# A two-block transformer kernel on one Trainium2 core: transfers, splits and sums of the opening in another order, and three small reorderings behind it

## What is computed

```python
def first_block(...):
    for layer in range(DEPTH):
        h = rmsnorm(x, attn_norm[layer])
        proj = h @ w_in[layer]
        y_a = diff_attention(a_q, a_k, a_v, cos, sin, ...) @ w_a[layer]
        y_b = hgrn2_bidirectional(b_q, b_ff, b_fb, b_i, b_g, ...) @ w_b[layer]
        merged = jax.nn.sigmoid(gate_a) * y_a + jax.nn.sigmoid(gate_b) * y_b
        x = x + merged @ w_o[layer]
        h = rmsnorm(x, ffn_norm[layer])
        x = x + (jax.nn.silu(h @ w_gate[layer]) * (h @ w_up[layer])) @ w_down[layer]
    return rmsnorm(x, final_norm)

def second_block(...):
    for l in range(DEPTH):
        x = layer_norm(ALPHA * x + 0.5 * swiglu(x, ...), ...)
        x = layer_norm(ALPHA * x + hybrid_mixer(x, ...), ...)
        x = layer_norm(ALPHA * x + 0.5 * swiglu(x, ...), ...)
```

## Time and profile before

| | us |
|---|---|
| median of 3 runs (lowest, highest) | 3565.53 (3564.04, 3565.78) |
| the profiled execution's own time | 3565.41 |
| its span in the profile | 3563.6 |
| PE busy in the span | 3506.7 |
| DVE busy | 1938.5 |
| ACT busy | 1382.6 |
| POOL busy | 463.4 |

### The profile page before, as it was taken

One profiled execution on the slowest core, in us unless ns is written; L12 is line 12 of the kernel. 1 busy time (PEld: TensorE's weight loads), 2 busy tenths in 40 slices (PEclk: granted clock), 3 DMA queues, 4 the chain that ended last, 5 costly groups with the idle time before them and its releaser, 6 DMA issues.

```text
span 3563.6 us, 44557 instructions
## 1 busy us (share of the span) xinstructions
PE 3506.7 (98%) x16012; PEld 2813.2 (79%) x16012; DVE 1938.5 (54%) x2485; ACT 1382.6 (39%) x1950; POOL 463.4 (13%) x320
## 2 busy tenths in 40 slices
PE   7999999999999999999999999999999999999998
PEld 5777888888777788888888876788878887678886
DVE  6888544434988654433443487633263328873334
ACT  4555433323455443323332355432242324653323
POOL 2333010001333110001200211200020003020002
PEclk9999999999999999999999999999999999999999
DMA  3111222223111222223222211222222222122222
GB/s 110 66 65 60 106 95 94 100 94 118 66 66 66 89 95 99 95 94 112 95 94 97 92 66 58 90 94 95 99 84 100 94 95 88 48 72 98 96 94 101
DMA packets 87378, 315.42 MB, mean 89 GB/s; under 512 B 9952, under 2 KB 10592, under 8 KB 86880
## 3 DMA queue, kind: packets, MB, share of 16 engines
q1 hardware_dynamic: 84384, 305.48, 25.2%
q10 hardware_dynamic: 2880, 8.39, 0.7%
HBM read 309.64 MB, written 4.19 MB: 88 GB/s over the span
## 4 chain that ended last, share of the span: by engine, by line
PE 87%; DVE 8%; DVEq 2%; ACT 2%; issue 1%; DMA 0%; POOLq 0%; SPq 0%; ACTq 0%; POOL 0%
PE ps L1760 22%; PE ps L1762 21%; PE ps L1761 21%; PE sc L1760 5%; PE sc L1762 5%; PE sc L1761 5%; DVE w_lo L1073 2%; PE ps L1928 1%; DVE h_lo L1520 1%; PE sc L2000 1%; DVEq L1378 1%; ACT w_hi L524 1%; DVEq L1544 1%; DVE DE L1307 1%; PE ps L1853 1%
## 5 line engine op out<-in xcount | busy, mean ns | idle before, releaser
L1073 DVE TENSOR_TENSOR w_lo<-raw,w_hi 128x1024 fp32r<-128x1024 f32 x574 | 738.7, 1287 | 1116.7 <-ACT w_hi L524 1116.4
L524 ACT ACTIVATE w_hi<-raw 128x1024 fp32r<-128x1024 f32 x574 | 607.9, 1059 | 1453.9 <-PE ps L1762 782.2
L1760 PE MATMUL ps<-h_hi,w_hi 128*128 128x512 f32 x2576 | 1049.1, 407 | 25.3 <-DVE h_lo L1083 23.2
L1762 PE MATMUL ps<-h_hi,w_lo 128*128 128x512 f32 x2576 | 1005.6, 390 | 0.0
L1761 PE MATMUL ps<-h_lo,w_hi 128*128 128x512 f32 x2576 | 1005.3, 390 | 0.0
L1760 PEld LDWEIGHTS ps<-h_hi,w_hi 128*128 128x128 f32 x2576 | 484.8, 188 | 154.8 <-issue 63.0
L1762 PEld LDWEIGHTS ps<-h_hi,w_lo 128*128 128x128 f32 x2576 | 484.0, 188 | 102.9
L1761 PEld LDWEIGHTS ps<-h_lo,w_hi 128*128 128x128 f32 x2576 | 485.4, 188 | 97.7 <-issue 9.1
L1760 PE MATMUL ps<-hid_hi,w_hi 128*128 (+1 forms) x792 | 309.7, 391 | 0.0
L1762 PE MATMUL ps<-hid_hi,w_lo 128*128 (+1 forms) x792 | 308.2, 389 | 0.0
L1761 PE MATMUL ps<-hid_lo,w_hi 128*128 (+1 forms) x792 | 308.2, 389 | 0.0
(11 more groups left out here) (314 smaller groups left out, 4337.5 us busy)
## 6 DMA issues: line engine op xcount, KB each, us to landing
raw<-wts SPq DMA_DIRECT2D x574, 512.0 KB, 3.2
x<-xT SPq DMA_DIRECT2D x1, 2048.0 KB, 10.6
x<-xT ACTq DMA_DIRECT2D x1, 2048.0 KB, 8.3
parked<-x ACTq DMA_DIRECT2D x8, 256.0 KB, 2.0
x<-parked ACTq DMA_DIRECT2D x1, 2048.0 KB, 8.1
outT<-x SPq DMA_DIRECT2D x8, 256.0 KB, 2.1
mask_in<-m ACTq DMA_DIRECT2D x1, 448.0 KB, 12.5
moves<-c ACTq DMA_DIRECT2D x1, 320.0 KB, 3.4
```

The source lines that it names most:

```text
L524: act(w_hi[:, s].rearrange("p a b -> p (a b)"), raw[:, s, :], ACT.Copy).then_inc(s_whi, 1)
L1073: tt(w_lo[:, s].rearrange("p a b -> p (a b)"), raw[:, s, :], w_hi[:, s].rearrange("p a b -> p (a b)").bitcast(F32), ALU.subtract).then_inc ...
L1760: mm(out, w_hi[:, s, b, :], hi, start=start, stop=False, skip_group_check=True)
L1762: return mm(out, w_lo[:, s, b, :], hi, start=False, stop=stop, skip_group_check=True)
```

## The change

Four parts. (a) Opening: the transfers are split up and in another order, chunk 0 in two halves, x in eight tiles on two queues, constants behind them; ACT and DVE split x and weights first and take squares, lower bounds and angles afterwards; the sum of squares is taken by PE behind chunk 2 and not behind chunk 1; four matmuls on a tile of zeros run first on PE, each 128x512 in float32. (b) The front of the first block's layers, on ACT and DVE, in another order. (c) The mixer's first scores on PE ahead of the transposes of v and three fill steps. (d) The mixer's end: the last splits, one centring and a few small steps at other pairs. Scratch tiles move: `mask_in` and four new `angle` tiles lie in space of the scan's tiles.

```diff
@@ sync
+            h0 = CHUNK // 2 * P
+            eng.dma_start(raw[:, 0, 0:h0], a_wts[0][:, 0:h0]).then_inc(s_half, 16)
             eng.dma_start(par1[:], a_par1).then_inc(s_first, 16)
-            eng.dma_start(x[:], a_x).then_inc(s_x, 16)
-            with eng.Fori(0, DEPTH * (CH1 + CH2) // 2 + 1) as pair:
+            eng.dma_start(raw[:, 0, h0:], a_wts[0][:, h0:]).then_inc(s_raw[0], 16)
+            eng.dma_start(x[:, 3, :], a_x[:, 3, :]).then_inc(s_x[3], 16)
+            eng.dma_start(raw[:, 1, :], a_wts[1]).then_inc(s_raw[1], 16)
+            for k in range(4, KT):
+                eng.dma_start(x[:, k, :], a_x[:, k, :]).then_inc(s_x[k], 16)
+            eng.dma_start(epsc[:], a_c1[:, 384:389]).then_inc(s_eps, 16)
+            eng.dma_start(ones[:], a_c1[:, 128:256]).then_inc(s_ones, 16)
+            eng.dma_start(sq[0][:].bitcast(I32), a_pos.partition_broadcast(P)).then_inc(s_pos, 16)
...
+            for s in range(2):
+                eng.wait_ge(s_wlo, 2 + s + 1)
+                eng.dma_start(raw[:, s, :], a_wts[2 + s]).then_inc(s_raw[s], 16)
+            eng.dma_start(scanm[:], a_c1[:, 389:901]).then_inc(s_const, 16)
...
+            with eng.Fori(2, DEPTH * (CH1 + CH2) // 2 + 1) as pair:
@@ scalar
-            eng.dma_start(ident[:], a_c1[:, 0:128]).then_inc(s_const, 16)
...
+            for k in range(3):
+                eng.dma_start(x[:, k, :], a_x[:, k, :]).then_inc(s_x[k], 16)
...
+                    eng.wait_ge(s_pre, 1)
+                    act(small[:, 16:32], small[:, 0:16], ACT.Exp).then_inc(s_sin, 1)
+                    split_hi(1, 1)
+                    eng.wait_ge(s_eps, 16)
+                    rstd_of(0, ps[7], D_MODEL, 0)
+                    split_hi(2, 0)
...
-                split_hi(p_proj + 2, 0)
-                split_hi(p_proj + 2, 1)
+                if L == 0:
+                    eng.wait_ge(s_pre, 2)
+                    act(sin1[:], angle[2][:], ACT.Sin)
+                    act(cos1[:], angle[3][:], ACT.Sin).then_inc(s_sin, 1)
+                    eng.preload_act_table_set("natural_log_exp_and_others")
                 front_exp(0)
...
                 split_hi(p_proj + 4, 0)
-                split_hi(p_proj + 4, 1)
                 decays(0, 0)
                 decays(0, 1)
+                split_hi(p_proj + 4, 1)
@@ scalar, mixer
                     if p == PAIRS - 1:
+                        for n in chunks_done_before(PAIRS):
+                            split_chunk(in0 + n + 2)
+                            take(n)
                         for i in range(2):
                             eng.wait_ge(q_ccx, L * 2 + i + 1)
@@ gpsimd
+            eng.memset(sT[:], 0.0).then_inc(s_warm, 1)
@@ vector
+                    eng.wait_ge(s_halfh, 1)
+                    tt(w_lo[:, 0, 0:half_k]..., raw[:, 0, 0:half_k * P], ...).then_inc(s_halfl, 1)
+                    eng.wait_ge(s_first, 16)
+                    for k in range(3):
+                        h_lo_of(0, k, k, ...)
+                    eng.wait_ge(s_whi, 1)
+                    tt(w_lo[:, 0, half_k:]..., raw[:, 0, half_k * P:], ...).then_inc(s_wlo, 1)
+                    for k in range(3, KT):
+                        h_lo_of(0, k, k, ...)
+                    split_lo(0, 1)
+                    bounds()
+                    turns()
+                    bounds_out()
...
+                split_lo(p_proj + 1, 0)
+                if L == 0:
+                    angles()
+                    split_lo(1, 1)
+                first(0, 0)
...
+                front_sums(0)
+                split_lo(p_proj + 2, 1)
+                first(1, 1)
...
+                front_decay(0)
                 first(2, 0)
                 split_lo(p_proj + 3, 0)
...
                 begin(0)
+                first(3, 1)
+                split_lo(p_proj + 4, 1)
@@ vector, mixer
                 for p in range(PAIRS + 1):
+                    if p == PAIRS - 1:
+                        for n in chunks_done_before(p):
+                            split_chunk(in0 + n + 2)
                     if p < PAIRS:
                         masked_max(p)
...
-                    if p < PAIRS:
-                        inverses(p)
-                    if p == 15:
-                        short_tap(1, 1)
-                        short_tap(1, 2)
-                        short_output(0)
+                    if p == PAIRS - 1:
                         eng.wait_ge(q_ccm, L + 1)
                         for i in range(2):
                             stt(cc[:, i, :], ps[6][:], -1.0 / 256, cc[:, i, :], ALU.mult, ALU.add).then_inc(q_ccx, 1)
-                    for n in chunks_done_before(p):
-                        split_chunk(in0 + n + 2)
+                    if p < PAIRS:
+                        inverses(p)
+                    if p == PAIRS - 2:
+                        short_tap(1, 1)
+                        short_tap(1, 2)
+                    if p == PAIRS - 1:
+                        short_output(0)
+                    else:
+                        for n in chunks_done_before(p):
+                            split_chunk(in0 + n + 2)
@@ tensor
-            eng.wait_ge(s_const, 96)
+            eng.wait_ge(s_warm, 1)
+            for _ in range(4):
+                mm(ps[7][:], sT[:, 0:P], sT[:], start=True, stop=True)
...
                 for s in range(2):
                     eng.wait_ge(s_wlo, (p_proj + 1) * 2 + s + 3)
                     chunk(ps[2 + s][:], s).then_inc(s_used, 1)
+                    if s == 0:
+                        if L == 0:
+                            proj_sums()
+                        eng.wait_ge(s_lam, L + 1)
+                        mm(ps[6][:, 0:2], ones[:], small[:, 34:36], ...).then_inc(s_lamp, 1)
@@ tensor, mixer
                 fill(2)
+                scores2(0)
                 eng.wait_ge(s_bank, bank0 + IN_TILES.index(T2_V) + 3)
                 transpose4(ps[7][:], row(M, T2_V)).then_inc(q_vTp, 1)
                 fill(FILLS2[0][0] - 2)
```

More of the change, by code:

```diff
@@ L220, in build @@
         stg = [tmp(f"stg{i}", 20 + i) for i in range(4)]
-        mask_in = tmp("mask_in", 24, 2)
+        mask_in = tmp("mask_in", 8, 2)
+        angle = [tmp(f"angle{i}", 10 + i) for i in range(4)]
         squared = [tmp(f"squared{i}", 20 + i) for i in range(KT)]
@@ L594, in gate_up, with first_high @@
                 eng.preload_act_table_set("natural_log_exp_and_others")
[L596 to L605, removed]
+            def first_high(k):
+                eng.wait_ge(s_x[k], 16)
+                act(h_hi[:, k, :], x[:, k, :], ACT.Copy, scale=par(par1, 0, C_AN + k)).then_inc(s_hhi, 1)
             eng.preload_act_table_set("natural_log_exp_and_others")
-            eng.wait_ge(s_x, 16)
             for L in range(DEPTH):
@@ L612, in _ @@
                 if L == 0:
-                    for k in range(KT):
[L614 to L620, removed]
+                    half_k = CHUNK // 2
+                    eng.wait_ge(s_half, 16)
+                    act(w_hi[:, 0, 0:half_k].rearrange("p a b -> p (a b)"), raw[:, 0, 0:half_k * P],
+                        ACT.Copy).then_inc(s_halfh, 1)
+                    eng.wait_ge(s_first, 16)
+                    for k in range(3):
+                        first_high(k)
+                    eng.wait_ge(s_raw[0], 16)
+                    eng.wait_ge(s_used, 1)
+                    act(w_hi[:, 0, half_k:].rearrange("p a b -> p (a b)"), raw[:, 0, half_k * P:],
+                        ACT.Copy).then_inc(s_whi, 1)
+                    for k in range(3, 6):
+                        first_high(k)
+                    split_hi(0, 1)
+                    for k in range(6, KT):
+                        first_high(k)
+                    for k in range(KT):
+                        square(s_x[k], 16, k, k)
+                        if k == 5:
+                            split_hi(1, 0)
+                    eng.wait_ge(s_pre, 1)
[5 more added lines that the diff above has]
+                else:
+                    statistics(2 * L, p_proj)
                 def front_exp(h):
@@ L1187, in _, with bounds @@
[L1187 to L1192 removed]
+            def bounds():
+                tt(small[:, 16:24], par1[:, 0, C_LBF:C_LBF + 8], par1[:, 1, C_LBF:C_LBF + 8], ALU.max)
+                eng.drain()
+                tt(small[:, 0:8], par1[:, 0, C_LBF:C_LBF + 8], small[:, 16:24], ALU.subtract)
+                tt(small[:, 8:16], par1[:, 1, C_LBF:C_LBF + 8], small[:, 16:24], ALU.subtract)
+                eng.drain()
+                eng.sem_inc(s_pre, 1)
@@ new lines, in turns @@
+            def turns():
+                eng.wait_ge(s_pos, 16)
+                eng.wait_ge(s_eps, 16)
+                eng.tensor_copy(sq[1][:], sq[0][:].bitcast(I32))
+                eng.drain()
+                ts(angle[0][:], sq[1][:], epsc[:, 2:3], None, ALU.mult)
+                eng.drain()
+                magic = 12582912.0
+                ts(angle[1][:], angle[0][:], float(np.float32(1 / (2 * math.pi))), magic, ALU.mult, ALU.add)
```

(20 more changed lines are left out.)

176 lines of the change are left out of this document (91 added, 85 removed).

## The result

| | us |
|---|---|
| before, median of 4 runs | 3565.61 (3564.04 to 3565.78) |
| changed, median of 4 runs | 3541.84 (3541.71 to 3542.13) |
| ratio | 0.9934, 95% interval 0.9917 to 0.9952 |
| span of the profiled execution, changed | 3539.9 (before 3563.6) |

The change gains 23.8 us. The forecast was 31.1, a median of 3534.5 with 3532 to 3537.5 as its likely band, and its range ended at 3542.0 on the slow side. That the median lies 0.16 us inside that end is luck: the opening, which carried most of the sum, gave 7.9 us of 17.3. The direction was right, and so were the mixers; in the opening a wait came back that the forecast had at 1.6 us.

A forecast was written before the change was run, and what follows sets the result against it. PE, busy 3506.7 of 3563.6 us, was taken as the bound. Terms 17.3 + 1.5 + 3.7 + 8.6 = 31.1 off 3565.41 gave 3534.3, with 3534.5 for the median; range 3529 to 3542.

The forecast's parts named there:

- (a): Opening: reordered transfers and splits start the first scan level at 64.2 instead of 81.50; 17.3 us, bounds 14 to 20.
- (b): Second layer's front: begin(0) ahead of the last take and split fills earlier waits; 1.5 us, bounds 0 and 1.5.
- (c): Mixers' first scores: issued earlier, they remove PE's waits for row maxima and small waits; 3.7 us, bounds 1.2 and 3.7.
- (d): Mixers' end: the 2.60 us wait and its slow stretch go in both layers; 8.6 us, bounds 5 and 8.6.
- Lower bounds and the first angle steps lie before 17.1: Opening, DVE: these steps are done before ACT's exponential of the lower bounds at 17.1; chunk 2 then begins at 20.9.
- The transfers: Opening: 3.2 MB up to tile 7 at 409 GB/s, 7.8 us from about 2 on, so landed at 10.
- PE's work from chunk 2 to the first scan level: Opening: PE's 42.8 us of work, as before, now begins at 20.9 and ends at 63.7.
- The cover for the squares: Mixer's end: ACT's squares come 2.9 us after the last chunk, while PE has about 3.3 us of work; cover 0.4 us.
- Transfers bound the opening: Rival, opening: tile 7 lands at 15, chunk 2 begins at 26, 3540; at 140 GB/s throughout 3550. Chance 0.10.
- DVE becomes the bound: Rival, ahead of the first scan level: both X waits stay, 1 to 3 us lost, 3538 to 3541. Chance 0.12.
- TensorE stays at 1.2 GHz: Rival: opening waits set the clock back and it stays; gain gone from 62 us, 80 us give 3574. Chance 0.02.
- my three signs of being wrong: Tile 7's h_hi starts after 12; PE waits over 2 us after 21; the squares' sum on PE waits for ACT.

The follow-up runs named there:

- the kernel with the wait of 2.39: Changed kernel with the low halves of chunks 2 and 3 moved on VectorE ahead of the short steps: 3535.6 us (3534.9 to 3536.3).

## Why the prediction was right where it was, and where it failed

**(a), 17.3 forecast, 7.9 measured: the step that failed.** It reads "Lower bounds and the first angle steps lie before 17.1." These steps stood behind a `w_lo` that was to end at 14.0, and GpSimd was to add from 13 on. I had the row that shows the cause, a `w_lo` of 2.08 us beside POOL against 1.21, and charged it to `w_lo` alone. The 3.1 us from 14.0 to 17.1 are enough for the lower bounds and the first angle steps only at the durations that they have with POOL idle, 2.7 us in all. Beside the sums the seven steps from 15.91 to 24.56 take 8.6 us where the run without the sums does them in 2.7 (15.48 to 18.15). Chunk 2 came at 27.69 and not at 20.9. The sums' cost is measured as a whole by leaving them out: 7.3 us, of which 1.7 is TensorE's half rate.

The Trainium skill (SBUF — State Buffer, Who interferes with whom) would have said so: a VectorE instruction contends with a GpSimd one that reads SBUF if it has two SBUF inputs, and so do copies, casts and tensor-scalar steps in the modes that use two ports; in these modes the one that issues first holds the shared ports for its whole instruction. The rows agree: the 128x8 steps with two inputs, the cast and the tensor-scalar steps take 1.27 to 1.51 us beside GpSimd's additions, which take 1.3 to 1.8 each, whatever their own length (one 128x8 step, at 17.26, slipped through in 0.17), and in the kernel with the low halves moved the addition at 18.33, beside a `w_lo`, took 2.38.

The balance of (a), which missed by 9.4 us: chunk 0 ended near 15.8 instead of 13.0 and chunk 1 at 21.8 instead of 19.3, 2.5; the wait behind it was 5.9 and not 1.6, 4.3; half rate 1.7; a wait for chunk 6's `w_lo` at 56.34, 1.0. Against that stand the 0.5 that I had set aside for chunk 4's bank and that were not needed. The sum is 9.0. The other 0.4 is PE's own work behind chunk 2, 43.2 instead of 42.8 (below).

**The transfers** were the smaller fault in (a). I had tile 7's `h_hi` done at 11.6, and it was at 14.0. The rate was 183 GB/s from 1.5 to 3.0, 393 from 6.0 to 9.0 and 343 as a mean from 2 to 11, not 409 throughout, and the half weights were in at 4.8 and not at 4. The 2.0 us for a tile "when alone" were of stores (`parked<-x`); in the opening the half weights took 5.0 us to land, and the tiles of x 4.5 on ScalarE's queue and 7.2 on SyncE's (medians). Ordering x ahead of the second chunk's weights gave 0.8 us, the third tile's place another 0.6, so order was part of it. The estimate that I had made from the table in the Trainium skill (DMA: Bandwidth & Descriptors, Bandwidth) was 230 GB/s for tiles of 256 KB. The trace has 393 with tiles and weights in flight together, so the measurement decides against that estimate here. The table is of loads issued from GpSimd and does not say how many were in flight; these came from SyncE and ScalarE.

**PE's work from chunk 2 to the first scan level**, 42.8 us, held: 45.9 from 27.69 to 73.61 less 1.7 and 1.0 is 43.2. That VectorE would have `X` in time held too: no wait, DVE at 8.39 of the last 10 us.

**(b)** 1.5 forecast, 1.8 by the traces, a little over its upper bound; no kernel of its own was run, so that it is the reordering is argued and not shown.

**(c)** 3.7 forecast, 3.7 by the medians, 5.1 by the spans. The mechanism was right. The upper bound was not safe: I took the sum of the waits that PE shows for it, and the traces have 0.7 more a mixer.

**(d)** 8.6 forecast, 8.7 by the medians, 8.8 by the spans. The cover for the squares held by 0.5 us, and PE does not wait for them (timeline of the changed kernel):

```profile
2177.45 1.14 ACT L993 ACTIVATE sc_padded<-cc_out 128x512 f32<-128x512 f32 x2
...
2179.13 1.99 PE L2385 MATMUL ps<-sc_padded,ones 128*128 128x512 f32 x4
```

**The rivals.** None came as written. "Transfers bound the opening" named 3540 and chunk 2 at 26, close to the 3541.8 and 27.69 that came, but by another way: the kernel with the low halves moved has the same transfers and took 3535.6. "DVE becomes the bound" named the right pair, VectorE beside POOL, but put it ahead of the first scan level, where both `X` waits were to stay, and priced it at 1 to 3 us. The real place was ahead of chunk 2, some 45 us earlier. "TensorE stays at 1.2 GHz" did not happen: the half rate ended by 31.56, after 3.9 us. Of my three signs of being wrong two were met: tile 7's `h_hi` started after 12, and PE waited over 2 us after 21.

## What to carry to other kernels

When work moves beside an engine that it did not run beside before, its old durations no longer hold; take them from a row with the same neighbour, and count each short step as held once. Three 128x8 steps took 2.7 us here, over twice a `w_lo` of 128x1024. So put what the bottleneck waits for ahead of the short steps in the queue of the engine that is held, and the short steps before the neighbour starts. And once the longest wait is gone, removing the next one can just show the one behind it: the bank wait of 1.41 us came back as 1.16 us some 13 us later, until the queue there was reordered too.

## What the runs showed that I had not expected

The half rate did not follow every wait. Behind the waits of 5.92 and 2.39 us the granted clock fell (0.58; 0.79 over eight us), behind those of 1.98, 1.66, 1.50 and 1.16 it stayed at 1.00; behind the mixer's 2.60 in the kernel before it was 0.56. In the kernel with the wait of 2.39 the matmuls at first ran at full rate: starts at 36.67, 36.98, 37.21 and 37.45, then 37.80 with 0.63 us each. The fall came when the work had already begun again. So it did behind the 2.60 us wait of the first mixer in the kernel before, after five matmuls; in the second mixer the matmuls were slow from the first.

The four products of zeros (eight records, 6.8 us of PE) set the rate of the first chunk's matmuls, 0.23 against 0.43 us, and changed the median by 0.3 us, within the scatter of the runs.
